# Feed-forward up-projection by seven half products in place of eight

## The chip, the cores and the metric

The kernel runs on one core of one Trainium2 chip. The metric is the time of one execution on the device in microseconds. A core has TensorE (PE in the profile, with its weight loads as PEld), VectorE (DVE), ScalarE (ACT), GpSimd (POOL) and SyncE (SP, which starts the DMA transfers here). They run side by side and wait for each other on semaphores.

## The reference

Two layers work on 128 prompt tokens and 512 sample tokens of width 1024. Layer 0 has an attention mixer, layer 1 a state-space mixer, and each ends in the same feed-forward block. The change is in that block.

```python
def rmsnorm(x, g): ...
def modulate(x, g, shift, scale): return rmsnorm(x, g) * (1 + scale) + shift

def conv_ffn(h, w_up, conv_w, conv_b, w_down):
    u = dwconv_centered(h @ w_up, conv_w, conv_b)     # 3 taps along the tokens
    g, v = jnp.split(u, 2, axis=-1)                   # gate and value, 2816 columns each
    return (jax.nn.silu(g) * v) @ w_down

for l in range(2):
    x = x + mod[2] * mixer(modulate(x, norm_mix_g[l], mod[0], mod[1]))
    x = x + mod[5] * conv_ffn(modulate(x, norm_ffn_g[l], mod[3], mod[4]), *ffn[l])
```

The six mod vectors of a layer come from a small product of the condition with ada_w (1024 x 6144, float32), which streams through the same core.

## The kernel before, in words

Activations are kept transposed: channels on the 128 partitions, tokens along the free dimension. xT is 8 such blocks of W = 642 columns (128 prompt, 2 pad, 512 sample). A matrix product in float32 is made of three products in float32r: each operand x is split in a high part (x rounded, `*_hi`) and a low part (x minus the high part, `*_lo`), and hi by hi, lo by hi and hi by lo are added up in PSUM.

**Up-projection.** 2816 gate and 2816 value columns of w_up are 22 tiles of 128 each (FT). Gate tile i and value tile i are a pair. A tile takes 8 blocks k of the 1024 inputs, 3 products, and 2 halves of the columns (324 and 318), so 48 matmuls; a pair takes 96. `steps` (L1060 to L1072, the matmul at L1069) issues them, two PSUM accumulators alternate. The 22 pairs come in three parts of 8, 8 and 6 pairs (PARTS), and after each part the down-projection of that part adds to xT: 8 output tiles of 8 (or 6) blocks k, 48 (or 36) matmuls each.

**Weights.** SP loads each tile of 512 KB in one of four buffers raw. POOL makes the high part (L1027, two instructions of 128x512) and then the low part (L1031, the same two) in one of two slots w_hi and w_lo; a slot is free when the tile two before it is done (mm_done), and PE waits for w_split.

**Input of the up-projection.** The kernel does not wait for the norm. While the last output tiles of the mixer are evacuated, ACT makes h_hi from x times the gain (L1645) and DVE makes h_lo (L2045); the reciprocal root mean square of each token is applied to the product, on DVE (L2072, ps times rbs), and the shift sits in the two pad columns, from which side columns and a bias for the convolution are made (L2077, L2390). So PE goes from the mixer's last tile straight to the first up tile, and the sum of squares (L1135) and the broadcast of the root (L1141, L1142) are issued between its matmuls.

**After a tile.** ACT makes the middle tap and bias (L1808), DVE adds the two other taps from PSUM (L2394, L2396). After a value tile ACT takes silu of the gate (L1812), DVE multiplies (L2404, hm), ACT rounds hm to g_hi (L1815) and DVE makes g_lo (L2406). The down-projection's tiles are added to xT by DVE (L2341).

**ada_w.** In layer 0 its rows are multiplied in bursts between parts: 4 steps (1 MB each) of 8 matmuls with 256 columns (L1112).

What sets the order of the work: each engine's program order and the semaphores. The up and down loops are hardware loops on all engines. The down tiles wait for f_ready, the up tiles for w_split and acc_free_dve.

## Time and profile before

| | |
|---|---|
| median of 3 runs | 1881.08 us (1880.3 to 1882.69) |
| profiled execution | span 1880.0 us (the page gives the span and no other time for it) |
| PE busy | 1815.3 us, 97% |
| PEld, POOL, DVE, ACT busy | 91%, 63%, 53%, 32% |
| mean granted TensorE clock | 0.991 of full |
| DMA | 208.66 MB, mean 111 GB/s |

Layer 0's feed-forward block lies between 309.0 and 803.3 us of the span, layer 1's between 1389.7 and 1865.2 us. Busy time of PE says that it always had a matmul in flight, not that it was at its peak; how fast it went is read from the distance between the starts of matmuls.

### The profile page before, as it was taken

The numbers are of one execution on the slowest core, as the hardware profiler recorded it, in microseconds if no ns is written. First come the engines' busy times: TensorE is split into PE (matmuls) and PEld (weight loads), VectorE is DVE, ScalarE is ACT, GpSimd is POOL, SyncE is SP. The second block draws the span as 40 slices with busy tenths as digits, with TensorE's granted clock in tenths as the row PEclk, the third lists the DMA queues.
The fourth block names the chain that finished last, engine by engine and source line by source line (L and its number), as shares of the span: only waits on it lengthen the run. The fifth ranks groups of instructions, "written<-read, shape, count | busy, mean of one in ns | idle before, by whom it ended". The sixth has DMA issues, their size and how long they took to land. (4 is left out here: it accounts for less than half of the span.)

```text
span 1880.0 us, 33251 instructions
## 1 busy us (share of the span) xinstructions
PE 1815.3 (97%) x12789; PEld 1713.1 (91%) x12789; DVE 994.1 (53%) x1589; ACT 602.4 (32%) x1149; POOL 1189.6 (63%) x869
## 2 busy tenths in 40 slices
PE   6999999999999999989999999989999999999997
PEld 5878799999999999979889898868999999999997
DVE  4556754662256236364666666587346623651552
ACT  4245421220022012143765856574112201220221
POOL 2533466777777777746555455534877778777774
PEclk9999999999999999989999999989999999999999
DMA  9631164424243424434333433243222222222212
GB/s 357 210 123 39 33 227 151 162 76 159 68 156 88 147 88 136 157 101 116 112 102 113 128 93 117 79 123 101 78 70 69 77 72 74 78 67 78 75 54 84
DMA packets 256188, 208.66 MB, mean 111 GB/s; under 512 B 7352, under 2 KB 235741, under 8 KB 255453
## 3 DMA queue, kind: packets, MB, share of 16 engines
q1 hardware_dynamic: 255373, 204.69, 34.6%
q10 hardware_dynamic: 720, 2.62, 0.4%
q8 instruction: 69, 1.13, 0.2%
q14 instruction: 26, 0.21, 0.0%
HBM read 196.63 MB, written 10.67 MB: 110 GB/s over the span
## 5 line engine op out<-in xcount | busy, mean ns | idle before, releaser
L1027 POOL TENSOR_SCALAR w_hi<-raw 128x512 fp32r<-128x512 f32 (+1 forms) x430 | 640.8, 1507 | 669.1 <-PE ps L1069 510.5
L1031 POOL TENSOR_TENSOR w_lo<-raw,w_hi 128x512 fp32r<-128x512 f32 (+1 forms) x430 | 548.6, 1297 | 0.0
L1069 PE MATMUL ps<-h_hi,w_hi 128*128 128x324 f32 (+1 forms) x1432 | 345.2, 322 | 2.9 <-DVE h_lo L2451 2.9
L1069 PE MATMUL ps<-h_hi,w_lo 128*128 128x324 f32 (+1 forms) x1432 | 329.0, 311 | 0.0
L1069 PE MATMUL ps<-h_lo,w_hi 128*128 128x324 f32 (+1 forms) x1432 | 327.6, 310 | 0.0
L1069 PEld LDWEIGHTS ps<-h_hi,w_hi 128*128 128x128 f32 x1432 | 241.4, 190 | 20.6 <-issue 20.3
L1069 PEld LDWEIGHTS ps<-h_hi,w_lo 128*128 128x128 f32 x1432 | 240.6, 189 | 0.0
L1069 PEld LDWEIGHTS ps<-h_lo,w_hi 128*128 128x128 f32 x1432 | 240.3, 189 | 0.0
L2341 DVE SCALAR_TENSOR_TENSOR xT<-ps,mod,xT 128x128 f32 (+1 forms) x112 | 56.6, 547 | 270.9 <-PE ps L1069 265.5
L1069 PE MATMUL ps<-g_hi,w_hi 128*128 128x324 f32 (+1 forms) x816 | 188.6, 312 | 5.0 <-POOL w_lo L1031 3.3
L1069 PE MATMUL ps<-g_hi,w_lo 128*128 128x324 f32 (+1 forms) x816 | 187.2, 310 | 0.0
L1069 PE MATMUL ps<-g_lo,w_hi 128*128 128x324 f32 (+1 forms) x816 | 186.2, 309 | 0.0
L1808 ACT ACTIVATE cg<-ps,small,par 128x130 f32<-128x130 f32 x88 | 49.8, 617 | 364.8 <-DVE small L2390 364.8
L1069 PEld LDWEIGHTS ps<-g_hi,w_hi 128*128 128x128 f32 x816 | 136.5, 189 | 8.8 <-issue 4.5
L1069 PEld LDWEIGHTS ps<-g_hi,w_lo 128*128 128x128 f32 x816 | 136.7, 189 | 0.0
L1069 PEld LDWEIGHTS ps<-g_lo,w_hi 128*128 128x128 f32 x816 | 136.6, 189 | 0.0
L1808 ACT ACTIVATE cv<-ps,small,par 128x130 f32<-128x130 f32 x88 | 49.8, 617 | 206.2 <-DVE small L2390 206.2
L2072 DVE TENSOR_TENSOR ps<-ps,rbs 128x642 f32<-128x642 f32 x88 | 73.0, 829 | 79.2 <-PE ps L1069 79.2
L1069 PE MATMUL ps<-h_c,w_hi 128*128 128x324 f32 (+1 forms) x440 | 100.7, 310 | 0.0
L1224 PE MATMUL ps<-h_hi,w_hi 128*128 128x318 f32 (+1 forms) x256 | 88.1, 344 | 1.4 <-issue 1.2
L1069 PE MATMUL ps<-h_b,w_hi 128*128 128x324 f32 x352 | 80.4, 310 | 0.0
L1069 PE MATMUL ps<-h_b,w_lo 128*128 128x324 f32 x352 | 80.2, 309 | 0.0
(372 smaller groups left out, 3087.2 us busy)
## 6 DMA issues: line engine op xcount, KB each, us to landing
raw<-in_ffn_w_up SPq DMA_DIRECT2D x88, 512.0 KB, 3.9
ada<-in_ada_w SPq DMA_DIRECT2D x40, 1024.0 KB, 6.4
raw<-in_ssd_w_in SPq DMA_DIRECT2D x40, 512.0 KB, 4.1
raw<-in_ffn_w_down SPq DMA_DIRECT2D x32, 512.0 KB, 3.9
R<-scr_acs SPq DMA_DIRECT2D x22, 512.0 KB, 4.9
raw<-in_att_w_in SPq DMA_DIRECT2D x16, 512.0 KB, 6.7
ada_att<-in_ada_w SPq DMA_DIRECT2D x8, 1024.0 KB, 7.0
raw<-in_ssd_w_out SPq DMA_DIRECT2D x16, 512.0 KB, 4.1
```

The costliest lines, as they stand in the source:

```text
L1027: nc.gpsimd.tensor_scalar(w_hi[slot][:, a_:b_, :], raw[j][:, a_:b_, :], 1.0, None, ALU.mult).then_inc(w_hi_done, 1)
L1031: ins = nc.gpsimd.tensor_tensor(w_lo[slot][:, a_:b_, :], raw[j][:, a_:b_, :], w_hi[slot][:, a_:b_, :].bitcast(F32), ALU.subtract)
L1069: ins = mm(out[:, cols], w[slot][:, k, :], x[:, cols], start=first and k == 0 and i == 0, stop=last and k == n - 1 and i == 2)
L1224: ins = mm(out, w[t % 2][:, k, :], x[:, cols], start=k == 0 and i == 0, stop=k == KD - 1 and i == 2)
L1808: ins = A_(buf[:, cols], acc(half)[:, cols], ACT.Identity, bias=small[:, b_:b_ + 1], scale=param_at(m + (wc + 44)))
L2072: step(tt(acc(slot), acc(slot), rrow(n)[:, :], ALU.mult))
L2341: ins = stt(x_, acc(slot)[:, cols], gate, x_, ALU.mult, ALU.add)
```

## The change

Each block is computed by one level of Strassen's scheme in Winograd's form. The 2x2 splits are: of the weights, gate or value tile by first or second 512 inputs; of the input, first or second 512 inputs by left or right half of the columns (HW = 322 of 644). The 8 half products (4 blocks k, 322 columns, 3 products: 12 matmuls) become 7, named 1 to 7. Products 1, 2 and 4 take weights as loaded, 5, 6, 7 and 3 take sums and differences of weights (`chain_1` to `chain_4` on DVE; the running sum is in PSUM, in st_ps). Products 1, 2, 3, 4, 5, 6, 7 take the input blocks b11, b21, b22, t4, t1, t2, t3, where t1 to t4 are sums and differences of quarters of the input (`combine`). Four more additions on DVE per pair put the products together (`up_left`, `up_sum`, `low_right`, `up_right`), with copies of products 1 and 5 made by ACT (`copy_p1`, `copy_p5`).

What moves with it:
- The input is normalised and shifted before it is used (`prepare`), in h32; the scaling of the product, its side columns and its bias (L2072, L2077, L2390) are gone.
- Work is in jobs of 12 matmuls (up) or 24 or 12 (half a down tile). Four weight slots of 4 blocks each go round; ACT rounds the high part of each job (`job_high`), POOL makes the low part (`job_lo`), DVE makes it for products 5 and 6.
- hm and g_lo are made by POOL (`hidden`, `hidden_low`).
- SP loads halves of tiles (256 KB).
- In layer 0, ada_w for 20 of the steps is multiplied inside products 1 and 2 of pairs 0 to 19 (`ada_side`), in matmuls of 128 columns; `side_add` on DVE collects them.
- All loops of the block are unrolled.

The diff, cut to its core:

```diff
+def ffn_schedule():
+    jobs = []
+    for p, (m0, n) in enumerate(PARTS):
+        jobs += [("P", 1, m0), ("P", 2, m0), ("P", 5, m0)]
+        for i in range(m0, m0 + n - 1):
+            jobs += [("P", 6, i), ("P", 1, i + 1), ("P", 2, i + 1), ("P", 7, i), ("P", 3, i), ("P", 5, i + 1),
+                     ("P", 4, i)]
+        i = m0 + n - 1
+        jobs += [("P", 6, i), ("P", 3, i), ("P", 7, i), ("D", p, 0, 0), ("P", 4, i), ("D", p, 1, 0), ("D", p, 2, 0),
+                 ("D", p, 0, 1), ("D", p, 1, 1), ("D", p, 2, 1)]
+        jobs += [("D", p, m, half) for m in range(3, KD) for half in range(2)]
+    return jobs
...
+            def job_lo(l, job):
+                j = JOB_AT[job]
+                nk = len(job_ks(job))
+                pool.wait_ge(job_hi, job_done(l, job))
+                nc.gpsimd.tensor_tensor(job_lo_home(j, nk), job_src(job), job_hi_home(j, nk).bitcast(F32), ALU.subtract
+                                        ).then_inc(lo_pool, 1)
...
+                for j in range(2):
+                    low_of(j)
+                for k in range(4):
+                    comb_low(n, "b21", slice(k, k + 1), h32[:, 4 + k:5 + k, 0:HW], 5 + k)
+                comb_low(n, "b22", slice(0, 4), h32[:, 4:8, HW:WS], 10)
+                comb_low(n, "t3", slice(0, 4), t32["t3"][:, :, :], 12)
+                comb_low(n, "t4", slice(0, 4), t32["t4"][:, :, :], 13)
+                for j, job in enumerate(JOBS):
+                    low_of(j + 4)
+                    if job[0] == "P":
...
+            def ada_side(i, j):
+                s = ADA_SIDE[i]
+                pe.wait_ge(ada0_in[4 * j], 16 * ADA_NTH[s][j])
+                for k in range(2):
+                    for q in range(4):
+                        ins = mm(side_out(i, j)[32 * q:32 * q + 32, :], sv_ffn[:, 2 * (s % 4) + k, :], side_in(j)[:, k, P * q:P * (q + 1)],
+                                 start=False, stop=k == 1, skip_group_check=True)
+                ins.then_inc(ada_mm, 1)
...
-                    def pair(i, peeled):
-                        for half in range(2):
-                            t = tp + 2 * i + half
-                            pe.wait_ge(w_split, t + 1)
-                            pe.wait_ge(acc_free_dve, dve_accs(ap) + 2 * i + half - 2)
-                            begins = peeled and p == 0
-                            def row(k, half=half):
-                                if half == 0 and k == 5:
-                                    ss(n_)
-                                if half == 1 and k == l:
-                                    norm_rb(n_)
-                            steps(half, half, h_of(n_), range(KD), ready=h_wait(n_) if begins and half == 0 else None,
-                                  after=row if begins else None).then_inc(mm_done, 1)
...
+            def product(l, x, i):
+                g, p = FT * l + i, part_of(i)
+                m0, n = PARTS[p]
+                j = JOB_AT["P", x, i]
+                out = px(i) if x in (1, 6, 7, 4) else py(i) if x == 2 else pz(i) if x == 3 else pv(i)
+                if x in (5, 6):
+                    pe.wait_ge(lo_dve, 2 * g + x - 4)
+                else:
+                    pe.wait_ge(lo_pool, lo_pool_done(l, ("P", x, i)))
+                if x in (1, 5):
+                    if i >= m0 + 2:
+                        pe.wait_ge(value_free, g - 1)
...
+                wh, wl = job_hi_home(j), job_lo_home(j)
+                ch, cl = c_hi[COMB_OF[x]], c_lo[COMB_OF[x]]
+                for k in range(4):
+                    if i == 0:
+                        comb_wait(l, x, k)
+                    for n_, (w, c) in enumerate(((wh, ch), (wh, cl), (wl, ch))):
+                        ins = mm(out, w[:, k, :], c[:, k, :], start=x in (1, 2, 3, 5) and (k, n_) == (0, 0),
+                                 stop=x in (2, 3, 4, 5) and (k, n_) == (3, 2), skip_group_check=True)
+                        if l == 0 and i in ADA_SIDE and x in (1, 2) and (k, n_) == (0, 0):
+                            ada_side(i, x - 1)
+                ins.then_inc(job_mm, 1)
...
+            def job_high(l, j):
+                job = JOBS[j]
+                if j >= 4:
+                    act.wait_ge(job_mm, l * N_JOBS + j - 3)
+                else:
+                    act.wait_ge(mm_done, (T_E, T_END)[l] - 1 + j // 2)
+                if job[0] == "P" and job[1] not in (1, 2, 4):
+                    act.wait_ge(s_sum, 4 * (FT * l + job[2]) + {5: 1 if job[2] else 2, 6: 4, 7: 3, 3: 4}[job[1]])
+                else:
+                    act.wait_ge(*landed(l, job))
+                A_(job_hi_home(j, len(job_ks(job))), job_src(job), ACT.Copy).then_inc(job_hi, 1)
...
+                def add_shift(k):
+                    act.wait_ge(hx_done, 8 * l + k + 1)
+                    for s_, cols in SEGS:
+                        ins = A_(h32[:, k, cols], h32[:, k, cols], ACT.Identity, bias=modc(l, 3, k, s_))
+                    ins.then_inc(h32_done, 1)
+                def high_of(name, ks, src):
+                    A_(c_hi[name][:, ks, :], src, ACT.Copy).then_inc(comb_hi, 1)
+                def high_t(name, n_):
+                    act.wait_ge(comb_32, 4 * l + n_)
+                    high_of(name, slice(0, 4), t32[name][:, :, :])
+                for k in range(4):
+                    add_shift(k)
+                    act.wait_ge(h32_done, 8 * l + k + 1)
+                    high_of("b11", slice(k, k + 1), h32[:, k:k + 1, 0:HW])
+                for k in range(4, 8):
+                    add_shift(k)
+                    act.wait_ge(h32_done, 8 * l + k + 1)
+                    high_of("b21", slice(k - 4, k - 3), h32[:, k:k + 1, 0:HW])
+                high_t("t1", 1)
+                high_of("b22", slice(0, 4), h32[:, 4:8, HW:WS])
+                high_t("t2", 2)
+                copy_p1(l, 0)
+                high_t("t3", 3)
+                high_t("t4", 4)
...
+                high_job(2)
+                root(turn_of(2 * l + 1) - 1)
+                high_job(3)
+                prepare(l)
+                copy_t(l, 1)
+                for j, job in enumerate(JOBS):
...
+                    if x == 4:
+                        value_id(l, i)
+                        if i + 2 < m0 + n:
+                            copy_t(l, i + 2)
+                        silu(l, i)
+                    high_job(j + 4)
+                    if x == 1 and i > m0 + 1:
+                        hidden_high(l, i - 2)
+                    if x == 7 and last:
+                        hidden_high(l, i - 1)
+                    if x == 1 and i:
+                        copy_p1(l, i)
+                    if x == 5:
+                        copy_p5(l, i)
+                    if x == 3:
...
+            def up_left(l, i):
+                dve.wait_ge(p1_copied, FT * l + i + 1)
+                dve.wait_ge(job_mm, job_done(l, ("P", 2, i)))
+                if l == 0 and i in ADA_SIDE:
+                    side_add(i)
+                tt(py(i), py(i), p1c, ALU.add).then_inc(c11_done, 1)
...
+            def normalise(l, k):
+                for s_, cols in RANGES:
+                    ins = stt(h32[:, k, cols], xT[:, k, cols], gain1[:, 2 * l + 1, k, s_:s_ + 1],
+                              bank(6, P) if s_ == 0 else bank(7), ALU.mult, ALU.mult)
+                    (step(ins) if s_ == 0 else ins.then_inc(hx_done, 1))
...
+                chain_1_low(l, 0)
+                dve.wait_ge(rb_done, turn_of(n))
+                for k in range(KD):
+                    normalise(l, k)
+                    if 1 <= k < 5:
+                        b11_low(l, k - 1)
                 if l == 0:
-                    ada_row_out(5)
-                step(stt(nws[:, :], par[:, wc:wc + 44], -1.0, par[:, wc + 44:wc + 88], ALU.mult, ALU.subtract))
-                step.wait()
-                step(tt(nws[:, :], nws[:, :], par[:, wc + 88:wc + 132], ALU.subtract))
-                root_row(n_)
+                    ada_row_out(5, 6, 2 * P)
+                dve.wait_ge(h32_done, 8 * l + 4)
+                combine(l, "t1", h32[:, lo4, right], h32[:, lo4, left])
+                chain_2_low(l, 0)
+                comb_low(l, "t1", lo4, t32["t1"][:, :, :], 9)
+                dve.wait_ge(h32_done, 8 * l + 8)
+                dve.wait_ge(comb_32, 4 * l + 1)
+                combine(l, "t2", h32[:, hi4, right], t32["t1"][:, :, :])
+                up_left(l, 0)
+                comb_low(l, "t2", lo4, t32["t2"][:, :, :], 11)
+                combine(l, "t3", h32[:, hi4, right], h32[:, lo4, right])
+                dve.wait_ge(comb_32, 4 * l + 2)
+                combine(l, "t4", h32[:, hi4, left], t32["t2"][:, :, :])
...
+            def period(l, i):
+                m0, n = PARTS[part_of(i)]
+                if i > m0:
+                    value_taps(l, i - 1)
+                if i + 1 < m0 + n:
+                    chain_1(l, i + 1)
+                    up_sum(l, i)
+                    chain_1_low(l, i + 1)
+                    chain_2(l, i + 1)
+                    up_left(l, i + 1)
+                    chain_3(l, i + 1)
+                    chain_4(l, i + 1)
+                    low_right(l, i)
+                    chain_2_low(l, i + 1)
+                    up_right(l, i)
...
```

How the order of instructions changes is shown at three places. First POOL, where layer 0's feed-forward block starts: before, its rows for a tile, where raw, w_hi and w_lo are the buffers of the weights.

```order
L1027 TENSOR_SCALAR w_hi_80<-raw_76 128x512 [waits mm_done,raw_in0,ones_done]
L1027 TENSOR_SCALAR w_hi_80<-raw_76 128x512
L1030 ISA
L1031 TENSOR_TENSOR w_lo_82<-raw_76,w_hi_80 128x512 [waits w_hi_done]
L1030 REGISTER_ALU
L1031 TENSOR_TENSOR w_lo_82<-raw_76,w_hi_80 128x512 [waits w_hi_done]
```

After; comb_107 to comb_113 are high parts and comb_114 to comb_120 low parts of b11, b21, t1, t2, t3, b22, t4, h_121 is h32, and s_126 and s_127 are the weight sums of products 7 and 3.

```order
L1199 TENSOR_TENSOR w_lo_82<-raw_76,w_hi_80 128x512 [waits job_hi] x2
L1205 TENSOR_TENSOR comb_115<-h_121,comb_108 128x322 [waits comb_hi] x4
L1205 TENSOR_TENSOR comb_119<-h_121,comb_112 128x1288 [waits comb_hi]
L1205 TENSOR_TENSOR comb_118<-t_t_124,comb_111 128x1288 [waits comb_hi]
L1205 TENSOR_TENSOR comb_120<-t_t_125,comb_113 128x1288 [waits comb_hi]
L1199 TENSOR_TENSOR w_lo_82<-raw_78,w_hi_80 128x512 [waits job_hi] x2
L1199 TENSOR_TENSOR w_lo_83<-s_126,w_hi_81 128x512 [waits job_hi]
L1199 TENSOR_TENSOR w_lo_83<-s_127,w_hi_81 128x512 [waits job_hi]
L1199 TENSOR_TENSOR w_lo_82<-raw_77,w_hi_80 128x512 [waits job_hi]
```

POOL no longer makes high parts. The low parts of the input blocks b21 (four instructions), b22, t3 and t4 stand between the weights of the first two jobs and the weights of the fifth and sixth job.

Second DVE, one value tile and the hidden product before.

```order
L2072 TENSOR_TENSOR ps<-ps,rbs 128x642 [waits mm_done]
L2077 COPY ps<-ps 128x2 [waits dve_step]
L2390 TENSOR_SCALAR small<-ps,nws,par 128x2
L2394 SCALAR_TENSOR_TENSOR cv<-ps,par,cv 128x642 [waits ffn_id]
L2396 SCALAR_TENSOR_TENSOR cv<-ps,par,cv 128x642 [waits dve_step]
L2404 TENSOR_TENSOR hm<-sg,cv 128x642 [waits acc_free_dve,ffn_silu]
L2406 TENSOR_TENSOR g_lo<-hm,g_hi 128x642 [waits ffn_hi]
```

After, the same stretch of one period in layer 1: taps of the value tile before, then weight chains of the next pair among additions of this one (tn_98 is the copy of product 1, diag that of product 5).

```order
L2773 SCALAR_TENSOR_TENSOR cv<-ps,par,cv 128x641 [waits id_value]
L2773 SCALAR_TENSOR_TENSOR cv<-ps,par,cv 128x641 [waits dve_step]
L2703 TENSOR_TENSOR ps<-ps,raw_77 128x512 [waits raw_in1,t_copied]
L2757 TENSOR_TENSOR su_128<-ps,diag 128x322 [waits job_mm,p5_copied]
L2709 TENSOR_TENSOR w_lo_82<-ps,w_hi_80 128x512 [waits job_hi]
L2721 TENSOR_TENSOR ps<-ps,raw_76 128x512 [waits raw_in0,lo_dve,s_sum]
L2751 TENSOR_TENSOR ps<-ps,tn_98 128x322 [waits job_mm,p1_copied]
L2730 TENSOR_TENSOR s_126<-raw_77,ps 128x512 [waits half_in1,lo_pool,s_sum]
L2737 TENSOR_TENSOR s_127<-raw_76,ps 128x512 [waits half_in0,lo_pool]
L2762 TENSOR_TENSOR ps<-ps,diag 128x322 [waits job_mm]
L2743 TENSOR_TENSOR w_lo_83<-ps,w_hi_81 128x512 [waits job_hi]
L2768 TENSOR_TENSOR ps<-ps,su_128 128x322 [waits job_mm,u4_done]
```

hm and g_lo left DVE; ten other operations stand between two sets of taps, and seven of them wait for a product (job_mm) or for a high part or copy by ACT (job_hi, t_copied, p1_copied, p5_copied).

Third PE, at the border of two up tiles before.

```order
L1069 MATMUL ps<-h_lo,w_hi_80 128x318
L1069 MATMUL ps<-h_hi,w_lo_82 128x324
L1069 MATMUL ps<-h_hi,w_lo_82 128x318
L1343 REGISTER_ALU
L1345 REGISTER_ALU [waits w_split]
L1069 MATMUL ps<-h_hi,w_hi_81 128x324 [waits acc_free_dve]
L1069 MATMUL ps<-h_hi,w_hi_81 128x318
L1069 MATMUL ps<-h_lo,w_hi_81 128x324
```

After, at the border of product 6 of a pair and product 1 of the next.

```order
L1608 MATMUL ps<-comb_110,w_hi_80 128x322
L1608 MATMUL ps<-comb_117,w_hi_80 128x322
L1608 MATMUL ps<-comb_110,w_lo_82 128x322
L1608 MATMUL ps<-comb_107,w_hi_80 128x322 [waits value_free,lo_pool]
L1608 MATMUL ps<-comb_114,w_hi_80 128x322
L1608 MATMUL ps<-comb_107,w_lo_82 128x322
L1608 MATMUL ps<-comb_107,w_hi_80 128x322
```

Product 1 of a pair starts with a wait for value_free, which the taps of the value tile two pairs before it give. That tile's last job, product 4, ends only one job (product 6 of the pair between) ahead of this wait.

## Rows read from the trace of the kernel before

**Rows 1.** The page: span, and busy time, share and instructions of each engine.
```profile
span 1880.0 us, 33251 instructions
...
PE 1815.3 (97%) x12789; PEld 1713.1 (91%) x12789; DVE 994.1 (53%) x1589; ACT 602.4 (32%) x1149; POOL 1189.6 (63%) x869
```

**Rows 2.** Windows of layer 1's block: busy by engine, PEclk, DMA share, GB/s.
```profile
1420.00:1828.00 408.00, 405.31 (x2743) 403.77 (x2742) 196.70 (x279) 75.23 (x124) 310.02 (x229) 1.00 0.25 73
```

**Rows 3.** Timeline of PE: layer 0's block begins; start us, us, engine, line.
```profile
309.13 3.66 PE L1112 MATMUL ps<-ada,tn 128*32 128x256 f32 x64
```

**Rows 4.** Timeline of PE: layer 1's first up tile.
```profile
1389.65 0.46 PE L1069 MATMUL ps<-h_a,w_hi 128*128 128x324 f32 x2
```

**Rows 5.** Timeline of PE: two successive up tiles, end of layer 1's block.
```profile
1564.04 0.45 PE L1069 MATMUL ps<-h_a,w_hi 128*128 128x324 f32 x2
...
1571.10 0.45 PE L1069 MATMUL ps<-h_a,w_hi 128*128 128x324 f32 x2
...
1865.16 0.93 PE L1597 MATMUL ps<-consts,xT 128*128 128x128 f32 x7
```

**Rows 6.** Timeline of DVE after an up tile.
```profile
1571.31 0.83 DVE L2072 TENSOR_TENSOR ps<-ps,rbs 128x642 f32<-128x642 f32 x1 [5.83 <-PE ps L1069]
```

**Rows 7.** Timeline of DVE at the end of layer 1's mixer, last residual.
```profile
1390.90 0.89 DVE L2690 TENSOR_TENSOR xT<-xT,tn 128x128 f32<-128x128 f32 x2
```

**Rows 8.** Waits of PE in layer 1's block: us, times, longest.
```profile
PE ps L1069 <- POOL w_lo L1031: 2.1, 3, 1.0
```

**Rows 9.** DVE groups by shape: count, busy us, mean ns, idle before.
```profile
L2394 DVE SCALAR_TENSOR_TENSOR cv<-ps,par,cv 128x642 f32<-128x642 f32 x44 | 39.0, 887 | 60.6 <-ACT cv L1808 60.6
...
L2632 DVE TENSOR_TENSOR R<-R,cbm 128x1024 f32<-128x1024 f32 x22 | 30.9, 1441 | 1.3 <-ACT R L1941 0.3
...
L2037 DVE TENSOR_TENSOR sums<-sums,sq 128x642 f32<-128x642 f32 x21 | 20.7, 987 | 0.5 <-ACT sq L1764 0.3
...
L2638 DVE TENSOR_TENSOR yg<-ps,yg 128x512 f32<-128x512 f32 x20 | 13.8, 689 | 19.3 <-PE ps L1532 19.2
...
L2188 DVE TENSOR_TENSOR qkv_raw<-ps,rrow_att 128x324 f32<-128x324 f32 x12 | 5.9, 496 | 15.0 <-PE ps L1224 10.9 <-DMA scr_x<-xT 4.0
```

**Rows 10.** ACT groups by shape.
```profile
L1812 ACT ACTIVATE sg<-cg 128x642 f32<-128x642 f32 x44 | 32.5, 738 | 0.0
...
L1941 ACT ACTIVATE R<-R 128x1024 f32<-128x1024 f32 x22 | 23.3, 1059 | 0.5
...
L1889 ACT ACTIVATE cx<-ps,par 128x642 f32<-128x642 f32 x16 | 14.2, 888 | 18.0 <-PE ps L1069 17.4
...
L1920 ACT ACTIVATE x_tok<-ps 128x512 f32<-128x512 f32 x16 | 9.5, 592 | 14.9 <-PE ps L1492 14.9
```

**Rows 11.** POOL group by shape.
```profile
L1031 POOL TENSOR_TENSOR w_lo<-raw,w_hi 128x512 fp32r<-128x512 f32 x398 | 516.9, 1320 | 0.0
```

**Rows 12.** Timeline of PE where layer 1's mixer waits for a norm.
```profile
803.44 3.66 PE L1112 MATMUL ps<-ada,tn 128*32 128x256 f32 x64
807.03 1.28 PE L1135 MATMUL ps<-ones,sums 128*128 128x1 f32 x10
...
815.72 0.88 PE L1069 MATMUL ps<-h_hi,w_hi 128*128 128x324 f32 x2 [2.86 <-DVE h_lo L2451]
```

**Rows 13.** Timeline of DVE there: first product with the root.
```profile
812.47 1.01 DVE L2460 SCALAR_TENSOR_TENSOR tn<-xT,gain,ps 128x128 f32<-128x128 f32 x2 [2.01 <-PE ps L1142]
```

**Rows 14.** Windows of 2 us there: busy by engine, PEclk third from the end.
```profile
818.00:820.00 2.00, 2.00 (x9) 1.87 (x8) 1.97 (x5) 1.02 (x2) 0.00 (x0) 0.50 0.00 0
820.00:822.00 2.00, 2.00 (x14) 1.91 (x13) 1.96 (x5) 1.02 (x2) 0.00 (x0) 0.85 0.00 0
```

**Rows 15.** Timeline of POOL and DVE at one hidden product.
```profile
1581.44 2.55 POOL L1031 TENSOR_TENSOR w_lo<-raw,w_hi 128x512 fp32r<-128x512 f32 x2
...
1582.73 1.94 DVE L2404 TENSOR_TENSOR hm<-sg,cv 128x642 f32<-128x642 f32 x1
```

**Rows 16.** Timeline of PE: a matmul pair after a wait, and the next.
```profile
1514.40 0.56 PE L1069 MATMUL ps<-g_hi,w_hi 128*128 128x324 f32 x2 [0.30 <-DVE g_lo L2406]
```

More of the change, by code:

```diff
@@ new lines, in home_of @@
+def home_of(load):
+    return (2 * (load[2] % 2) + 1, 0) if load[1] == "21" else block_of(load)
+LOADS = ffn_loads()
+LOAD_AT, LOAD_OLD, _held, _count = {}, {}, {}, {}
+for _load in LOADS:
+    _home = home_of(_load)
+    _count[_home] = _count.get(_home, 0) + 1
+    LOAD_AT[_load] = _count[_home]
+    LOAD_OLD[_load] = _held.get(_home)
+    _held[_home] = _load
+LOADS_PER = dict(_count)
+ADA_SIDE = {i: 24 + i for i in range(20)}
+ADA_TURNS = ((6, 7), (8, 9), (10,))
+ADA_BUF = {s: s % 5 for s in range(8)}
@@ L921, in row_loads @@
+            ffn(0)
+            for b in range(4):
+                sp.wait_ge(lo_pool, lo_pool_done(0, ("D", 2, 4 + b, 1)))
             def row_loads(n, d_):
@@ new lines, in _, with ffn @@
+            ADA_READY = (6, 8, 10)
+            def ffn(l):
+                if l == 0:
+                    ada_steps(range(21, 23), o=2 * P)
+                ss(2 * l + 1)
+                if l == 0:
+                    ada_steps((23,), o=2 * P)
+                norm_rb(2 * l + 1)
+                for job in JOBS:
+                    if job[0] == "P":
+                        product(l, *job[1:])
+                        if l == 0 and job[1] == 6 and job[2] == 0:
+                            ada_turn(5, 2).then_inc(ada_cols, 1)
+                        continue
+                    _, p, m, half = job
+                    down(l, p, m, half)
+                    if l == 0 and (m, half) == (3, 1):
+                        pe.wait_ge(dn_free, 8 * p + 3)
+                        for row in ADA_TURNS[p]:
+                            ada_turn(row, 2, 2 * P * (row % 2)).then_inc(ada_cols, 1)
@@ L2436, in ffn @@
+            def ffn(l):
+                prepare(l)
+                for p, (m0, n) in enumerate(PARTS):
+                    for i in range(m0, m0 + n):
+                        period(l, i)
+                    downs(l, p)
                 if l == 0:
[L2437 to L2439 removed]
+                    add_square(2, 7, sq[1])
+            ffn(0)
             root_row(2)
```

944 lines of the change are left out of this document (568 added, 376 removed).

## The prediction, before the result was known

> **What bounds the kernel now.** I read the page first. PE is busy 97% of a span of 1880.0 us, every other compute engine at most 63% [rows 1]. A share is a mean over stages, so the second view is the window of layer 1's feed-forward block: PE 405.3 of 408 us at full clock, DVE 196.7, ACT 75.2, POOL 310.0, and DMA at 0.25 of its time [rows 2]. The third is the list of waits: in that whole block PE's costliest wait is 2.1 us, for a low part of the weights [rows 8]. So PE alone sets the time there. From the starts of two successive tiles, 1564.04 and 1571.10, a tile of 48 matmuls takes 7.06 us, so 0.147 us per matmul of about 321 columns and 14.13 us per pair [rows 5]. The blocks take 803.44 − 309.13 = 494.3 us in layer 0 [rows 3, 12], with six bursts of ada_w of some 3.7 us inside, and 1865.16 − 1389.65 = 475.5 us in layer 1 [rows 4, 5]. Only less work on PE, or work on it that goes faster, can gain; whatever makes PE wait costs in full.
>
> **The change, part by part**
>
> **Fewer matmuls.** A pair has 84 in place of 96. 44 × 12 × 0.147 = 77 us go. A pair is now 84 × 0.1475 = 12.4 us (322 columns each).
>
> **Preparation.** Before, PE's first up tile stood right behind the mixer's last one. Now all input passes through a norm, a shift and sums first, and PE stands idle meanwhile. I follow it from tE, the end of PE's last mixer tile in layer 1 (1389.65 [rows 4]).
> - The last residual ends at 1391.8 [rows 7], tE + 2.1. Two squares added (0.97 each, [rows 9], L2037 987 ns) with a weight chain of 0.69 (L2638) between put the sum of squares at tE + 4.9. From there to the first product with the root took 812.47 − 807.03 = 5.4 us before [rows 12, 13], so DVE normalises from tE + 10.4.
> - Per block, ACT adds the shift (1.02, from 888 ns for 642 columns and a second small piece) and makes a high part of 322 columns (0.47, on the line through 592 ns for 512 and 1059 for 1024) [rows 10]: 8 × 1.5 = 12 us, so b21 is done at tE + 23.4. Products 1 and 2 follow and end at about tE + 19 and + 25.
> - t1 needs all of this, then a high part (1288 columns, 1.3) on ACT and a low part (1.4) on DVE: product 5 from tE + 26. b22's low part goes to POOL: 1.32 us per 512 [rows 11], 3.2 for 1288. t2 follows (sum 1.4, high 1.3, low 1.4): product 6 from tE + 32 to 34.
> - Then PE wants product 1 of pair 1, whose low part stands on POOL behind the low parts of b22, t3 and t4. t3 and t4 are sums that wait for t2 on DVE; two more low parts of 3.2 and one weight part of 1.3 behind them put its start at tE + 42.3 to 44.5. I take 43.5. In layer 0 the mixer's residual has fewer steps: 42.4.
>
> Until then PE has done products 1, 2, 5, 6: 48 × 0.1475 = 7.1 us of work. After idling it runs slow, too: in the norm between the layers it waited from 807 to 815.7 us and the granted clock was 0.50 in the window 818 to 820 and 0.85 in the next [rows 12, 14]. About 4.5 us of matmuls at half speed cost 2.2 us per layer. So preparation costs about 43.5 + 2.2 − 7.1 = 38.6 us in layer 1, less the 3 us or so that PE already lost around there before. It is the largest term against the change.
>
> Whether t2 waits for b22's low part hangs on the two engines in front of one memory. Before, POOL's 2.55 us at 1581.44 and DVE's hidden product from 1582.73 overlapped: DVE's ended only 0.68 us after POOL's, and took 1.94 [rows 15] where a similar DVE operation takes 0.89 to 0.99 [rows 9]. I let the two take turns. The Trainium skill says the same in "SBUF — State Buffer", section "SBUF: two separate sides": a DVE operation with two operands in SBUF and a GpSimd operation hold the port they share exclusively, and the other one waits. The row agrees (1.94 us for an operation of 0.99). By that rule preparation is at the upper end, 44.5; if they didn't exclude each other it would be 41.6, and the sum 4 to 6 us lower over both layers.
>
> **A new wait per pair.** Product 1 of pair i writes where value tile i − 2 was. Between that tile's last product (4) and product 1 of pair i stands product 6 alone, 12 × 0.1475 = 1.77 us. In that time ACT must read the tile (value_id, 0.888 [rows 10]) and DVE add two taps (0.887 each [rows 9]), with 0.21 us before the first (DVE's row starts at 1571.31, PE's next tile at 1571.10 [rows 5, 6]) and 0.1 for the hops: 0.21 + 0.89 + 1.77 + 0.1 = 2.98. PE waits 1.2 us, and about 0.15 goes in the restart (a pair of matmuls took 0.56 after a wait, else 0.46 [rows 16]): 1.35. The wait exists from the third pair of each part on: 6 + 6 + 4 = 16 per layer, 21.6 us per layer. Queued behind the waiting matmul is all of PE; in its shadow DVE and ACT gain time.
>
> **The other engines.** Per period of 12.4 + 1.35 = 13.75 us, from counts of the changed kernel times the nearest row: DVE four chains and two low parts of 512 columns (0.69 each), four additions of 322 (0.49 each) and four taps (0.89 each): 9.7 to 10.0; ACT 9.0 to 9.3; POOL five low parts of 1.32 and hm and g_lo with 642 columns, 1.6 each in proportion: 9.6 to 9.9 [rows 11]. All are under 13.75 as sums. But they depend on each other in turn: value_id, copy, silu and a high part on ACT; two low parts and hm on POOL; g_hi and the copy of product 1 on ACT; the chains on DVE with a high part by ACT between. Added up, the round is 14.5 to 15.0 us, while product waits leave it 13.7 + 0.9. I count it hidden and keep the excess for a rival. The weights come in halves, the bytes stay, and DMA was busy a quarter of the time [rows 2]: no cost. The low parts after the last pair of a part lie under down jobs: no cost. POOL's hm and g_lo sit behind its own low parts; I count the 2.1 us wait of before [rows 8] as unchanged.
>
> **ada_w in layer 0.** The bursts of 3.66 us go. Each was 32 matmuls of 256 columns, two records in the trace for a matmul, so 3.66/64 = 57 ns per record [rows 12]. Instead 20 pairs get 16 matmuls of 128 columns, 32 records. No row has such a one. In proportion to columns a record costs 28.6 ns, at worst 57 ns like one of 256 columns: 0.92 to 1.83 us per pair. I take the middle, 1.38, as neither row is near, so 20 × 1.38 = 27.6, and 1.8 for the turns of other rows of ada_w. The Trainium skill ("TensorE: Matmul & The Clock Gate", section "Wait — 56ns, not 53.3ns?") gives a floor of about 25 ns between starts, however small the matmul. By it 128 columns may go at the proportional price, and the sum would be 9 us lower. By columns, 57 ns for 256 becomes 28.6 ns for 128, above that floor; the trace has nothing smaller than 256 columns to show it.
>
> **Sum.** The rest of the work, after the four first jobs, is 22 pairs of 84 matmuls less those 48, 1800 × 0.1473, and the down tiles, 1056 × 0.1475, together 420.9 us per layer.
> - Layer 1: 43.5 + 2.2 + 420.9 + 21.6 = 488.2, before 475.5: +12.7.
> - Layer 0: 42.4 + 2.2 + 420.9 + 21.6 + 27.6 + 1.8 = 516.5, before 494.3: +22.2.
> - Total +34.9 on the profiled span of 1880.0: 1914.9. The median of the runs is 1.1 above that span, so 1916.0.
>
> **Rivals**
>
> *The round of the other engines sets the period.* If it really is 14.5 us and nothing of it overlaps further, the period is 0.75 longer: 32 × 0.75 = 24 us, 1940. For it: the sum of single durations is already at or above the period, and shared ports only lengthen operations [rows 15]. Against it: the engines have 4 us idle each per period, and a stall of PE releases them. Chance 0.22.
>
> *Preparation is shorter.* If POOL reaches product 1 of pair 1 by the end of product 6, at about tE + 36, each layer saves 7.5: −15, 1901. For it: durations for t1 to t4 are interpolated. Against: POOL's order is fixed, and three low parts of 3.2 are in front. Chance 0.15.
>
> *The value tile is free in time, and the kernel gets faster.* If copy and taps fit under product 6, all 32 waits go: −43, 1873. It decides at a wait below 1.35 − 35/32 = 0.26 us per pair. Against it: 0.888 + 0.887 + 0.887 = 2.66 us [rows 9, 10] alone is more than 1.77. Chance 0.08.
>
> *The change gives all of its 77 us.* Without idle time at the start and without waits, and with ada_w as before, less 6 us: 1880 − 77 − 6 + 1, 1798. The order of POOL and the norm speak against it. Chance 0.03.
>
> **How the numbers follow.** My forecast has 0.52; there preparation at 41.6 to 44.5 makes ±3 and ada_w ±9, so its own range is 1903 to 1928. The first rival reaches to 1940, the second to 1901 and less with cheap ada_w: 1892. I take 1892 to 1942 for 8 in 10. About 0.2% (3.8 us) can be told from no change: faster 0.11 (the last two rivals), within it 0.04 (their border), slower 0.85.
>
> **What would show it.** In the windows at each block's start: PE busy 7 us of the first 43, then a clock of 0.50. In the waits: PE's product matmul waiting for DVE's second tap, some 32 times, about 1.2 us. In the block: 0.147 us between matmul starts, and PE periods of 13.75 us. In ada_w's lines: 28 to 57 ns per record of 128 columns. I am wrong if PE's longest idle stretch ends with another releaser than POOL's low part, if value waits are absent, or if periods differ from 13.75 by more than 0.3.

## The result, and the profile after

The changed kernel takes 1926.53 us (median of 4 runs, 1925.06 to 1928.79), the kernel before 1880.69 us beside it. The ratio is 1.0243, with a 95% interval of 1.0229 to 1.0258: slower by 46 us. The forecast was 1916, and the measured time lies in its range.

The page of the changed kernel, rows as in [rows 1]:

```profile
span 1923.6 us, 32461 instructions
...
PE 1787.4 (93%) x12581; PEld 1661.4 (86%) x12581; DVE 1045.7 (54%) x1765; ACT 891.8 (46%) x1640; POOL 1013.2 (53%) x743
```

PE is busy for 28 us less, and the span is 43.6 us longer. DVE's and ACT's share rose, POOL's fell. Here is what PE's product matmul (L1608) waited for in the whole run: us in all, times, longest.

```profile
PE ps L1608 <- DVE cv L2773: 37.1, 32, 2.3
PE ps L1608 <- DVE comb L2825: 17.7, 10, 4.3
PE ps L1608 <- POOL w_lo L1199: 12.4, 2, 6.3
```

The first row is the wait for the value tile, 32 times; the rest is the preparation of the input, which ended for PE in a wait for POOL's low part of the weights. Next the timeline of PE (start us, us, engine, line, operation, and in brackets the idle time before it and what ended it) at the ends of the blocks, in order: the ada_w steps right behind layer 0's mixer, those right behind its feed-forward block, the last matmuls of layer 1's mixer, and what follows its block.

```profile
311.17 1.93 PE L1326 MATMUL ps<-ada,tn 128*32 128x256 f32 x32
...
830.68 3.66 PE L1326 MATMUL ps<-ada,tn 128*32 128x256 f32 x64
...
1415.14 0.45 PE L1287 MATMUL ps<-y_hi,w_lo 128*128 128x324 f32 x2
...
1909.00 0.93 PE L1866 MATMUL ps<-consts,xT 128*128 128x128 f32 x7
```

With the same boundaries in [rows 3, 4, 5, 12], the 43.6 us divide like this:

| stretch | before | after | difference | forecast |
|---|---|---|---|---|
| up to layer 0's block | 309.1 | 311.2 | +2.0 | 0 |
| layer 0's block | 494.3 | 519.5 | +25.2 | +22.2 |
| layer 1's mixer | 586.2 | 584.8 | -1.4 | 0 |
| layer 1's block | 475.5 | 493.6 | +18.1 | +12.7 |
| the rest | 14.8 | 14.6 | -0.2 | 0 |

(The mixer's end is the start of its last matmuls plus 0.30, the distance from one such pair to the next.)

### The profile page after: what moved, and what is told of

It is laid out like the page before. It is cut to its first block and busy times, and to the rows that moved or that the text cites. A ratio compares the mean times of both kernels' runs of the same rounds, so it can differ in the third digit from the quotient of the medians.

```text
span 1923.6 us, 32461 instructions
## 1 busy us (share of the span) xinstructions
PE 1787.4 (93%) x12581; PEld 1661.4 (86%) x12581; DVE 1045.7 (54%) x1765; ACT 891.8 (46%) x1640; POOL 1013.2 (53%) x743
## 5 line engine op out<-in xcount | busy, mean ns | idle before, releaser
L1608 PE MATMUL ps<-comb,w_hi 128*128 128x322 f32 x2464 | 578.9, 320 | 70.0 <-DVE cv L2773 37.1
L1608 PEld LDWEIGHTS ps<-comb,w_hi 128*128 128x128 f32 x2464 | 427.2, 194 | 94.7 <-issue 76.9
L1181 POOL TENSOR_SCALAR w_hi<-raw 128x512 fp32r<-128x512 f32 x158 | 244.5, 1565 | 429.7 <-PE ps L1287 261.3
L1199 POOL TENSOR_TENSOR w_lo<-raw,w_hi 128x512 fp32r<-128x512 f32 (+1 forms) x228 | 285.1, 1254 | 308.1 <-ACT w_hi L2038 307.8
L1608 PE MATMUL ps<-comb,w_lo 128*128 128x322 f32 x1232 | 389.9, 317 | 0.0
L1608 PEld LDWEIGHTS ps<-comb,w_lo 128*128 128x128 f32 x1232 | 238.4, 193 | 0.0
L1185 POOL TENSOR_TENSOR w_lo<-raw,w_hi 128x512 fp32r<-128x512 f32 x158 | 207.2, 1332 | 0.0
L1287 PE MATMUL ps<-h_hi,w_hi 128*128 128x324 f32 (+1 forms) x640 | 162.2, 335 | 3.3 <-DVE h_lo L2941 3.3
L1287 PE MATMUL ps<-h_hi,w_lo 128*128 128x324 f32 (+1 forms) x640 | 147.2, 311 | 0.0
L1287 PE MATMUL ps<-h_lo,w_hi 128*128 128x324 f32 (+1 forms) x640 | 146.4, 310 | 0.0
```

The costliest lines, as they stand in the source:

```text
L1181: nc.gpsimd.tensor_scalar(w_hi[slot][:, a_:b_, :], raw[j][:, a_:b_, :], 1.0, None, ALU.mult).then_inc(w_hi_done, 1)
L1185: ins = nc.gpsimd.tensor_tensor(w_lo[slot][:, a_:b_, :], raw[j][:, a_:b_, :], w_hi[slot][:, a_:b_, :].bitcast(F32), ALU.subtract)
L1199: nc.gpsimd.tensor_tensor(job_lo_home(j, nk), job_src(job), job_hi_home(j, nk).bitcast(F32), ALU.subtract).then_inc(lo_pool, 1)
L1287: ins = mm(out[:, cols], w[slot][:, k, :], x[:, cols], start=first and k == 0 and i == 0, stop=last and k == n - 1 and i == 2)
L1608: ins = mm(out, w[:, k, :], c[:, k, :], start=x in (1, 2, 3, 5) and (k, n_) == (0, 0), stop=x in (2, 3, 4, 5) and (k, n_) == (3, 2), skip_ ...
```

## The experiments

Each is the changed kernel with an edit, timed beside the kernel before; times are compared by medians. Where a gain lies is read from the profiled executions: the start of PE's sum of squares (L1359 in the changed kernel) marks each block's start, and the next one, or the end of the span, its end.

| kernel | median | layer 0's block | mixer of layer 1 | layer 1's block to the end |
|---|---|---|---|---|
| the change | 1926.5 | 519.9 | 585.6 | 503.8 |
| `swap` | 1912.6 | 506.3 | 589.5 | 501.0 |
| `hh` | 1924.8 | 520.0 | 588.1 | 501.5 |
| `swap_hh` | 1883.6 | 501.0 | 587.9 | 479.3 |
| `prep` | 1923.2 | 515.5 | 588.7 | 502.1 |
| `both` | 1904.3 | 500.6 | 586.0 | 500.1 |
| `best` | 1869.5 | 494.8 | 587.5 | 471.4 |
| `side_one` | 1918.0 | 511.7 | 587.5 | 503.9 |
| `best_side` | 1860.8 | 485.9 | 589.5 | 471.4 |

The mixer between the blocks, which no edit touches, moves by up to 4 us from one profiled execution to the next.

### `swap`: products 1 and 2 in the other order

```diff
-            jobs += [("P", 6, i), ("P", 1, i + 1), ("P", 2, i + 1), ("P", 7, i), ("P", 3, i), ("P", 5, i + 1),
+            jobs += [("P", 6, i), ("P", 2, i + 1), ("P", 1, i + 1), ("P", 7, i), ("P", 3, i), ("P", 5, i + 1),
```

(`hidden_high` and `hidden_low` are issued beside the product that stands in the same place.)

> Products 1 and 2 of the next pair change places, so that products 6 and 2 (24 matmuls, 3.56 us) stand between product 4 and the product 1 that waits for the value tile. Theory A (value tile alone sets the period): copy and two taps need 2.98 us, the 32 waits of 1.12 us and their restarts go, the period of a pair in layer 1 falls from 13.86 to about 12.5 us, and the time from 1926.5 to about 1884. Rival B (the round of ACT, POOL and DVE, 14.5 us by single durations, is just behind it): PE waits under other names, the period stays above 13.5 us, and less than 12 us is gained.

Measured: 1912.6 us, ratio to the kernel before 1.0161 (1.0144 to 1.0178). So 14 us less, where 42 were expected. All waits for cv are gone, yet in layer 1 almost nothing was gained. The timeline of PE, the waits of two pairs in layer 1:

```profile
1506.35 0.53 PE L1608 MATMUL ps<-comb,w_hi 128*128 128x322 f32 x2 [0.93 <-DVE cg L2773]
...
1519.80 0.54 PE L1608 MATMUL ps<-comb,w_hi 128*128 128x322 f32 x2 [0.42 <-POOL w_lo L1199]
...
1533.88 0.54 PE L1608 MATMUL ps<-comb,w_hi 128*128 128x322 f32 x2 [0.90 <-DVE cg L2773]
```

Two pairs take 1533.88 - 1506.35 = 27.5 us, 13.77 each, against 13.86 in the changed kernel. PE now waits for the gate tile and for POOL's low part (in other pairs for an addition too, L2762), none of them long. What sets 13.77 is read by going back from a wait. Here ACT in the same stretch:

```profile
1506.23 0.74 ACT L2148 ACTIVATE sg<-cg 128x642 f32<-128x642 f32 x1
1506.88 1.14 ACT L2038 ACTIVATE w_hi<-s 128x512 fp32r<-128x512 f32 x2
...
1511.71 0.74 ACT L2154 ACTIVATE g_hi<-hm 128x642 fp32r<-128x642 f32 x1 [2.20 <-POOL hm L1216]
...
1512.87 0.42 ACT L2109 ACTIVATE tn<-ps 128x322 f32<-128x322 f32 x1
1515.11 0.60 ACT L2038 ACTIVATE w_hi<-ps 128x512 fp32r<-128x512 f32 x1 [1.81 <-DVE s L2737]
...
1516.92 0.89 ACT L2129 ACTIVATE cg<-ps,par 128x642 f32<-128x642 f32 x1 [0.70 <-issue]
...
1519.84 0.74 ACT L2148 ACTIVATE sg<-cg 128x642 f32<-128x642 f32 x1
```

and POOL:

```profile
1507.57 2.57 POOL L1199 TENSOR_TENSOR w_lo<-s,w_hi 128x512 fp32r<-128x512 f32 x2 [1.59 <-ACT w_hi L2038]
1510.10 1.57 POOL L1216 TENSOR_TENSOR hm<-sg,cv 128x642 f32<-128x642 f32 x1
```

It is a round: silu (1506.23), two high parts (1506.88), POOL's two low parts (1507.57) and then hm (1510.10), g_hi on ACT only when hm is there (1511.71), behind it the copy of product 1 (1512.87), for which DVE's `up_left`, `chain_3` and `chain_4` wait, then a high part (1515.11), the gate's copy (1516.92), and the next silu at 1519.84. The idle times on ACT and POOL end with the step before, on another engine (the profile names none for the 0.70 us before the gate's copy). This round takes 13.61 us; the starts of silu in layer 1 are 13.61 and 13.92 us apart in turn, 13.77 in the mean. That is the forecast's first rival, with a round of 13.77 us in place of 14.5 to 15.0, only 0.1 us behind the wait for the value tile. In layer 0 a pair takes longer on PE anyway (ada_w), so the round holds it up less there, and its block is 13.6 us shorter; layer 1's only 2.8.

### `hh` and `swap_hh`: the copy of product 1 ahead of g_hi

```diff
-                    if x == 1 and i > m0 + 1:
-                        hidden_high(l, i - 2)
...
                     if x == 1 and i:
                         copy_p1(l, i)
+                    if x == 1 and i > m0 + 1:
+                        hidden_high(l, i - 2)
```

This shortens the round: the copy no longer waits for hm. First alone, with the products in the order of the changed kernel:

> The changed kernel with one step moved: ACT copies product 1 before, not after, it rounds the hidden product (so the copy does not wait for POOL's hm). Product order as in the changed kernel. Theory A (the wait for the value tile alone sets the period there, the round over ACT, POOL and DVE is only just behind): nothing changes, 1925 to 1928, waits of 1.12 us stay. Rival B (the round sets the period and the value wait only shows it): the round is up to 2.4 us shorter and the time falls by 10 us or more.

Measured: 1924.8 us, ratio 1.0228 (1.0212 to 1.0243), which can't be told from the changed kernel (1.0229 to 1.0258). PE's waits are as before:

```profile
1505.26 0.54 PE L1608 MATMUL ps<-comb,w_hi 128*128 128x322 f32 x2 [1.12 <-DVE cv L2773]
...
1519.13 0.54 PE L1608 MATMUL ps<-comb,w_hi 128*128 128x322 f32 x2 [1.12 <-DVE cv L2773]
```

The period is 1519.13 - 1505.26 = 13.87 us. So there the value tile sets it. Then both edits:

> Products 1 and 2 changed in order, and the same step moved. Theory A (with the value wait gone, the round silu, two high parts, two low parts, hm, g_hi, copy of product 1, additions, gate copy sets 13.77 us per pair): without hm and g_hi in it the round is up to 2.4 us shorter, layer 1 goes at 12.6 to 12.9 us per pair, layer 0 at some 14.0, and the time falls from 1912.6 to about 1888. Rival B (another wait, for the gate tile or a low part, is as close): the period stays above 13.4 and the time above 1905.

Measured: 1883.6 us, ratio 1.0009 (1.0000 to 1.0018). Theory A held; it came out 4 us better than expected. The window of PE alone in this kernel (us, busy time and matmul records, PEclk, DMA share, GB/s), and two successive starts of silu on ACT, which mark a pair:

```profile
1650.00:1710.00 60.00, 60.00 (x407) 1.00 0.31 91
```

```profile
1651.08 0.73 ACT L2148 ACTIVATE sg<-cg 128x642 f32<-128x642 f32 x1
...
1663.55 0.73 ACT L2148 ACTIVATE sg<-cg 128x642 f32<-128x642 f32 x1
```

PE has no wait at all, and a pair takes 1663.55 - 1651.08 = 12.47 us, so its 84 matmuls take 0.1485 us each. (The 407 records of the window count those in flight at its two ends, so 60/407 would be too short.) So in the changed kernel the wait of 1.12 us and its restart cost 13.86 - 12.47 = 1.39 us per pair. The two edits gave 13.9 and 1.7 us alone, and 42.9 together: in layer 1 two limits of nearly the same height lay over each other, and each hid the other. Between the pairs of layer 0 five waits for ada_w's DMA are left, 0.1 to 1.0 us each, 2.5 together; this is the longest:

```profile
441.46 0.65 PE L1347 MATMUL ps<-ada,tn 128*32 128x128 f32 x16 [0.97 <-DMA ada<-in_ada_w]
```

### `prep`, `both`, `best`: the order on POOL in the preparation

```diff
-                comb_low(n, "b22", slice(0, 4), h32[:, 4:8, HW:WS], 10)
+                low_of(4)
+                low_of(5)
+                comb_low(n, "b22", slice(0, 4), h32[:, 4:8, HW:WS], 11)
                 comb_low(n, "t3", slice(0, 4), t32["t3"][:, :, :], 12)
                 comb_low(n, "t4", slice(0, 4), t32["t4"][:, :, :], 13)
```

(And the same two high parts before b22, t3 and t4 on ACT; the loop behind leaves both out.)

> At the start of each block, ACT and POOL make high and low parts of the weights of jobs 5 and 6 (products 1 and 2 of the second pair) before the high and low parts of b22, t3 and t4. Theory A (POOL's fixed order sets product 1 of the second pair): it starts some 32 us after the mixer's last tile in place of 43.7 and 42.1, each block is 8 to 11 us shorter, the time is about 1906. Rival B: the low part of t3 is late anyway and product 7 of the first pair takes over the wait; then PE's idle time only moves and less than 4 us per block is gained.

Measured: 1923.2 us, ratio 1.0216 (1.0199 to 1.0233), 3 us less. Rival B held. PE in layer 1, product 6, then product 7:

```profile
1447.11 0.88 PE L1611 MATMUL ps<-comb,w_hi 128*128 128x322 f32 x2 [2.50 <-DVE comb L2830]
...
1460.33 0.90 PE L1611 MATMUL ps<-comb,w_hi 128*128 128x322 f32 x2 [4.90 <-POOL w_lo L1199]
```

Products 1 and 2 of the next pair now follow product 6 without a wait, but product 7 waits 4.90 us for POOL, whose weight part stands behind b22, t3 and t4. The first order's long wait only moved by two products. In the changed kernel it was at product 1 of the second pair:

```profile
1459.11 0.90 PE L1608 MATMUL ps<-comb,w_hi 128*128 128x322 f32 x2 [6.29 <-POOL w_lo L1199]
```

1459.11 is 43.7 us behind the mixer's end, where 43.5 was forecast.

`both` has the edits of `swap` and of `prep`.

> Both reorderings together. If they are independent, their gains add up: about 42 and 20 us off 1926.5, so about 1864, below the 1880.7 of the kernel before. Rival: with the waits for the value tile gone, POOL and DVE have no slack to catch up with the delayed input parts and the sum is 10 us or more short of that, near 1875 to 1885.

Measured: 1904.3 us, ratio 1.0128 (1.0107 to 1.0149). By the medians this is 22.2 us less, where the two alone gave 13.9 and 3.3. In the two blocks of the profiled executions the gains add up (13.6 + 2.8 and 4.4 + 1.7, together 22.5, against 19.3 + 3.7 = 23.0); the mixer of layer 1 was 3 to 4 us longer in the executions of `swap` and `prep`. The expectation missed by 40 us, for the reasons that showed in each alone: the round still set the period, and product 7 still waited. Here is POOL in that kernel in layer 1, after the weight parts of jobs 5 and 6:

```profile
1430.27 3.96 POOL L1205 TENSOR_TENSOR comb<-h,comb 128x1288 fp32r<-128x1288 f32 x1
1434.18 7.05 POOL L1205 TENSOR_TENSOR comb<-t_t,comb 128x1288 fp32r<-128x1288 f32 x2
1441.19 2.52 POOL L1199 TENSOR_TENSOR w_lo<-s,w_hi 128x512 fp32r<-128x512 f32 x2
```

b22's low part took 3.96 us, while DVE made the sums t3 and t4 in the same memory, and those of t3 and t4 took 7.05 together, the first of them beside the end of DVE's t4; the weight parts of products 7 and 3 came last, at 1441.19. The next kernel puts each weight part where its product needs it (ACT's high parts move likewise), with the two edits of `swap_hh` in it:

```diff
+                low_of(4)
                 comb_low(n, "b22", slice(0, 4), h32[:, 4:8, HW:WS], 10)
+                low_of(5)
+                low_of(6)
                 comb_low(n, "t3", slice(0, 4), t32["t3"][:, :, :], 12)
+                low_of(7)
                 comb_low(n, "t4", slice(0, 4), t32["t4"][:, :, :], 13)
```

> As swap_hh, and at the start of a block POOL makes the low parts of the weights of jobs 5, 6, 7 and 8 between the low parts of b22, t3 and t4, each where the job needs it. Theory A (POOL's order, now with product 7 in view): product 7 of the first pair starts some 6 us earlier than with the first reordering, 8 us per block are gained against swap_hh, about 1873, below the kernel before at 1880.7. Rival B (POOL and DVE hold each other up in the same memory, so their summed work sets the end and the order doesn't matter): under 3 us per block, above 1882.

Measured: 1869.5 us, ratio 0.9932 (0.9919 to 0.9946): 14.1 us less than `swap_hh`, 6.2 and 7.9 in the two blocks. Product 7 of layer 1 starts 36.4 us behind the sum of squares, against 41.3 in `prep` and 44.5 in `swap_hh`: 4.9 us earlier than with the first reordering, where some 6 were expected. Theory A held; the order on POOL did matter, and this kernel is faster than the one before.

### `side_one`, `best_side`: ada_w inside the products

> Leaves out 7 of 8 matmuls of every group of ada_w inside products 1 and 2 of layer 0 (4 records of 32 per pair stay). Theory A (a record of 128 columns costs some 36 ns, and about 0.2 us per group goes on switching to it and back): 28 x 36 ns x 20 = 20 us gained, about 1906, and 0.5 us of 1.53 per pair stays. Rival B (all of it is by record, 48 ns): 27 us gained. Rival C (mostly the switch): under 10 us gained.

```diff
-                for k in range(2):
-                    for q in range(4):
+                for k in range(1, 2):
+                    for q in range(3, 4):
```

This kernel leaves out most of ada_w, so it only measures. Measured: 1918.0 us, ratio 1.0193 (1.0176 to 1.0210), 8.6 us less. By the number that is rival C; how the price divides is another matter, as `best_side` shows. First PE in the changed kernel, then in this one, product 1 of two successive pairs of layer 0:

```profile
401.05 0.39 PE L1608 MATMUL ps<-comb,w_hi 128*128 128x322 f32 x1 [1.12 <-DVE cv L2773]
401.37 0.64 PE L1347 MATMUL ps<-ada,tn 128*32 128x128 f32 x16
401.94 0.42 PE L1608 MATMUL ps<-comb,w_hi 128*128 128x322 f32 x1
...
416.44 0.38 PE L1608 MATMUL ps<-comb,w_hi 128*128 128x322 f32 x1 [1.12 <-DVE cv L2773]
```

```profile
399.08 0.39 PE L1608 MATMUL ps<-comb,w_hi 128*128 128x322 f32 x1 [1.12 <-DVE cv L2773]
399.40 0.41 PE L1347 MATMUL ps<-ada,tn 128*32 128x128 f32 x2
399.73 0.41 PE L1608 MATMUL ps<-comb,w_hi 128*128 128x322 f32 x1
...
413.99 0.39 PE L1608 MATMUL ps<-comb,w_hi 128*128 128x322 f32 x1 [1.12 <-DVE cv L2773]
```

A pair takes 15.39 us there and 14.91 here, where 13.86 is the time without ada_w (layer 1). So the 28 records left out were worth 0.48 us, and the 4 that stay, with two switches, still cost 1.05 us. In the first fence the matmul at 401.05 is followed by its neighbour not after 0.15 but after 0.89 us. A part of the price is by group. The last kernel takes that up:

```diff
-                        if l == 0 and i in ADA_SIDE and x in (1, 2) and (k, n_) == (0, 0):
-                            ada_side(i, x - 1)
+                        if l == 0 and i in ADA_SIDE and x in (1, 2) and (k, n_) == (0, 0):
+                            if i == m0:
+                                ada_side(i, x - 1)
+                            elif x == 1:
+                                ada_side(i, 0)
+                                ada_side(i, 1)
```

> As best, with both groups of ada_w of a pair in product 1 (all pairs but the first of a part). Theory A (a group costs some 0.5 us by the switch to it and back, hardly by its records): one switch less in 17 pairs, 17 x 0.4 = 7 us faster than best. Rival B (cost by record): no change within 2 us.

Measured: 1860.8 us, ratio 0.9885 (0.9870 to 0.9901), 8.7 us less than `best`. This does not come from the switches alone. Two successive groups in `best`, then in this kernel:

```profile
390.31 0.65 PE L1352 MATMUL ps<-ada,tn 128*32 128x128 f32 x16
...
404.32 0.64 PE L1352 MATMUL ps<-ada,tn 128*32 128x128 f32 x16
```

```profile
391.73 1.08 PE L1352 MATMUL ps<-ada,tn 128*32 128x128 f32 x32
...
405.41 1.08 PE L1352 MATMUL ps<-ada,tn 128*32 128x128 f32 x32
406.43 0.42 PE L1613 MATMUL ps<-comb,w_hi 128*128 128x322 f32 x1
```

An undisturbed pair takes 14.01 us there and 13.68 here. So a switch is worth 0.33 us, 5.6 for the 17 that went. Most of the other 3 us are waits for the DMA of ada_w: PE has these in `best` between 345 and 830 us (us in all, times, longest), and none in this kernel:

```profile
PE ps L1352 <- DMA ada<-in_ada_w: 2.3, 4, 1.2
```

The rest of a group's price is by record. From the start of a group to the next product's matmul it is 0.57 us with 16 records (401.37 to 401.94) and 1.02 with 32 (405.41 to 406.43): 28 ns for each of the 16. That `side_one` seems to give 17 ns (0.48 us for 28) has its reason in how they start. The same 32 records, counted in two windows (us, busy time and records, PEclk, DMA share, GB/s):

```profile
405.40:405.44 0.04, 0.03 (x4) 1.00 0.05 13
405.40:405.65 0.25, 0.24 (x8) 1.00 0.07 20
```

Four have started within 0.04 us, one for each of the four column ranges of the array, and only eight in 0.25 us. So they start four at a time, and each four takes (1.02 - 0.57)/4 = 0.11 us. A group of 16 is four such fours; the 2 records that `side_one` leaves in a group are one in each of two fours, so only two fours went, 0.24 us. This is the fastest kernel of the study, 1.15% faster than the kernel before.

## Why the prediction held, and where it was short

**Fewer matmuls.** 12.4 us of work per pair: 12.47 measured, once nothing else waited. That is 0.1485 us for a matmul, where the sum took 0.1473: 1800 of them make 2.2 us more per layer.

**Preparation.** Product 1 of the second pair was forecast at 43.5 and 42.4 us behind the mixer's end. It came at 1459.11 - 1415.44 = 43.7, and in layer 0 at 353.18 - 311.17 = 42.0, both waiting for POOL's weight part as said. The clock then, windows of 2 us in layer 1 and a window of 4 us with a later drop (PEclk third from the end, as in [rows 14]):

```profile
1460.00:1462.00 2.00, 2.00 (x10) 2.00 (x9) 0.00 (x0) 0.00 (x0) 2.00 (x3) 0.50 0.04 8
1462.00:1464.00 2.00, 2.00 (x13) 2.00 (x13) 0.64 (x1) 0.93 (x2) 0.79 (x1) 0.81 0.00 0
1490.00:1494.00 4.00, 4.00 (x19) 4.00 (x18) 0.95 (x3) 1.04 (x2) 3.25 (x3) 0.57 0.00 0
```

That is 0.50 and then 0.81, close to the 0.50 and 0.85 of [rows 14]: half speed until about 1462.8, which costs 1.8 us where 2.2 were forecast. The two engines took turns: DVE's sum t2 in layer 0, with POOL's low part of b22 beside it, and the sum t3, which ran alone:

```profile
335.38 3.99 DVE L2831 TENSOR_TENSOR t_t<-h,t_t 128x1288 f32<-128x1288 f32 x1
...
343.25 1.49 DVE L2831 TENSOR_TENSOR t_t<-h 128x1288 f32<-128x1288 f32 x1
```

```profile
335.17 2.84 POOL L1205 TENSOR_TENSOR comb<-h,comb 128x1288 fp32r<-128x1288 f32 x1 [1.58 <-ACT comb L2082]
```

t2 took 3.99 us where t3 took 1.49, and ended 1.36 us after POOL's operation, so it hardly moved while that ran. That is the turn-taking of [rows 15], and it fits POOL's longer low parts in the experiment above (3.96 us for b22 there, 2.84 here). So this step was right to the microsecond. What it left open was what is late next: with two jobs moved ahead on POOL, product 7 waited instead, and only with all four moved, on top of `swap_hh`, did 14 us come back.

**The wait per pair.** 32 waits of DVE's second tap, 31 of them of 1.12 to 1.19 us, forecast 1.2 and 1.35 with the restart; 1.39 measured with it. One of them in layer 1 was longer:

```profile
1489.68 0.56 PE L1608 MATMUL ps<-comb,w_hi 128*128 128x322 f32 x2 [2.33 <-DVE cv L2773]
...
1505.07 0.53 PE L1608 MATMUL ps<-comb,w_hi 128*128 128x322 f32 x2 [1.12 <-DVE cv L2773]
...
1518.92 0.53 PE L1608 MATMUL ps<-comb,w_hi 128*128 128x322 f32 x2 [1.12 <-DVE cv L2773]
```

At 1489.68 PE had waited 2.33 us. DVE was still at the gate's taps when the value tile's copy was there:

```profile
1485.77 2.06 DVE L2773 SCALAR_TENSOR_TENSOR cg<-ps,par,cg 128x322 f32<-128x322 f32 x4 [1.25 <-ACT cg L2129]
```

Product 4 had ended at about 1489.68 - 2.33 - 1.78 = 1485.57, so the value taps could have begun at 1486.7, and these ran to 1487.8. Then the granted clock was 0.57 for 4 us (fence above), and the next period was 15.39 us in place of 13.85. That is 1.2 + 1.5 = 2.7 us that no term of the sum held. (In `hh`, where the round is shorter, this wait is 1.12 us too, and layer 1's block 2.3 us shorter.) With the 2.2 us of the longer matmuls, 16 x 0.04 = 0.6 for the waits and 0.2 for the preparation, less 0.4 for the clock, this is 5.3 of the 5.4 us by which layer 1's block was longer than forecast.

**The other engines.** The sum of single durations gave 14.5 to 15.0, and the forecast called it hidden. At 13.86 it was hidden, by 0.1 us. The estimate was too long because it added durations, and successive operations of an engine start before the one ahead ends: silu starts at 1506.23 for 0.74 us and the next starts 0.65 later (ACT's rows of the first experiment); a tenth of a us at each of some ten steps. That this is all of the difference was not followed step by step. As a reading of what bounds the kernel, "hidden" was right; as a statement of what there is to gain it would have misled: removing the wait alone gave 0.09 us per pair in layer 1.

**ada_w.** 1.38 us per pair was forecast, 15.39 - 13.86 = 1.53 measured, near enough by luck. The forecast had no term for the switch and put a record between 28.6 and 57 ns. The runs show 28 ns a record, its lower price, so 0.9 us for 32, and 2 x 0.33 us for the switches; the middle that it took stood in for a cost that it did not name. The forecast also priced 20 pairs, but the groups of pair 0 lie in the preparation, where PE waits anyway. So 19 x 1.53 = 29.1 us stand against 27.6. With 2.2 for the longer matmuls and 0.6 for the waits, less 0.4 in the preparation and 0.4 for the clock, that makes 3.5 us, and layer 0's block was 3.0 us longer than forecast; the 0.5 between was not followed. The Trainium skill ("TensorE: Matmul & The Clock Gate", section "Wait — 56ns, not 53.3ns?"), weighed in the forecast, has starts never closer than about 25 ns. In the mean the trace agrees, with 28 ns a record; but four records that go to four column ranges start within 0.04 us (windows of `best_side`), so between those the floor does not hold here, and the measurement decides.

**Not foreseen:** 2.0 us ahead of layer 0's block. About one of them is a group of 16 records of ada_w that now stands inside the mixer; for the other, the granted clock between 200 and 250 us was 0.97, in the kernel before 1.00. The tables show that stretches without an edit differ by as much.

## What to carry to other kernels

When a wait ends last in a periodic stage, compute what the dependency round over the other engines takes before pricing the wait's removal: here it was 0.1 us shorter, and two edits worth 14 and 2 us alone were worth 43 together. In an engine's fixed order, place each operation where its consumer needs it; moving the first two consumers' operations only moved the wait to the third. Small foreign matmuls inside a dense stream cost 0.33 us for each interruption here besides their own time, so group them; and before a whole gain is put down to one cause, compare undisturbed periods: of the last 8.7 us some 3 lay elsewhere, 2.3 of them in waits for DMA.
